# Scoring the first two heads of the second attention together on one NeuronCore

## The reference

```
def _fox_attend(q, k, v, log_f):
    c = jnp.cumsum(log_f, axis=1)
    ...
        s = jnp.einsum('bqhd,bkhd->bhqk', q_b, k, ...) * (d ** -0.5)
        s = s + cq_b[..., :, None] - ck[:, :, None, :]
        s = jnp.where(kpos[None, :] <= qpos[:, None], s, NEG_INF)
        w = jax.nn.softmax(s, axis=-1).astype(v.dtype)
        return jnp.einsum('bhqk,bkhd->bqhd', w, v)
```

## Time and profile before

| | us |
|---|---|
| median of three runs | 2059.25 |
| lowest and highest | 2057.09, 2059.43 |
| the profiled execution, whole | 2058.62 |
| its span, first to last instruction | 2056.8 |

### The profile page before, as it was taken

How to read it: one execution, slowest core, us unless ns; L and a number is a source line. 1 busy time by engine, 2 the same in 40 slices (tenths; PEclk the granted TensorE clock), 3 DMA queues, 4 the chain that set the end, 5 groups by cost and what they waited for, 6 DMA issues and landing times.

```text
span 2056.8 us, 24737 instructions
## 1 busy us (share of the span) xinstructions
PE 1984.4 (96%) x9280; PEld 1643.0 (80%) x9280; DVE 884.6 (43%) x1218; ACT 307.3 (15%) x596; POOL 1281.9 (62%) x831
## 2 busy tenths in 40 slices
PE   9889999999997999999999999998999899999998
PEld 8778778888886878888788888876787778888886
DVE  3468182243338510373642343375458950000234
ACT  1048120000003100263300000031221120000001
POOL 5488566667764555785576667755453456666675
PEclk9999999999999999999999999999999999999999
DMA  6310333232332222212233223232221123323332
GB/s 209 123 42 1 92 93 102 92 101 93 99 116 62 83 92 83 72 43 71 82 113 100 94 94 101 92 103 72 75 80 54 55 89 95 100 92 101 92 100 74
DMA packets 53410, 181.31 MB, mean 88 GB/s; under 512 B 6553, under 2 KB 9291, under 8 KB 53211
## 3 DMA queue, kind: packets, MB, share of 16 engines
q1 hardware_dynamic: 46512, 165.17, 25.6%
q10 hardware_dynamic: 6826, 15.11, 2.2%
HBM read 176.56 MB, written 3.70 MB: 88 GB/s over the span
## 4 chain that ended last, share of the span: by engine, by line
PE 81%; DVE 11%; POOL 5%; ACT 1%; issue 1%; DMA 0%; POOLq 0%; DVEq 0%
PE PS L571 79%; PE PS L728 1%; POOL WL L483 1%; DVE X L1373 1%; DVE X L1374 1%; POOL WH L480 1%; DVE X L1335 1%; DVE STL L1590 1%; PE PS L793 1%; POOL AQL L489 1%; POOL AKL L489 1%; DVE XTL L1364 1%; POOL PB L512 1%; DVE OT L1619 1%; DVE X L1435 0%
## 5 line engine op out<-in xcount | busy, mean ns | idle before, releaser
L480 POOL TENSOR_SCALAR WH<-RW 128x1024 fp32r<-128x1024 f32 x303 | 359.3, 1186 | 697.0 <-PE PS L571 654.9
L483 POOL TENSOR_TENSOR WL<-RW,WH 128x1024 fp32r<-128x1024 f32 x303 | 770.6, 2543 | 25.3
L571 PE MATMUL PS<-XTH,WH 128*128 128x512 f32 x1168 | 458.4, 392 | 5.5 <-POOL WL L483 2.6
L571 PE MATMUL PS<-XTL,WH 128*128 128x512 f32 x1168 | 456.0, 390 | 0.0
L571 PE MATMUL PS<-XTH,WL 128*128 128x512 f32 x1168 | 455.7, 390 | 0.0
L571 PE MATMUL PS<-WL,HSH 128*128 128x512 f32 x688 | 267.5, 390 | 2.1 <-POOL WL L483 2.1
L571 PE MATMUL PS<-WH,HSH 128*128 128x512 f32 x688 | 267.7, 389 | 0.0
L571 PE MATMUL PS<-WH,HSL 128*128 128x512 f32 x688 | 267.7, 389 | 0.0
L571 PEld LDWEIGHTS PS<-XTH,WH 128*128 128x128 f32 x1168 | 219.9, 188 | 54.3 <-DVE XTL L1364 3.9
L571 PEld LDWEIGHTS PS<-XTH,WL 128*128 128x128 f32 x1168 | 220.0, 188 | 46.4
L571 PEld LDWEIGHTS PS<-XTL,WH 128*128 128x128 f32 x1168 | 220.2, 188 | 44.5
(11 more groups left out here) (311 smaller groups left out, 2364.0 us busy)
## 6 DMA issues: line engine op xcount, KB each, us to landing
RW<-stream SPq DMA_DIRECT2D x303, 512.0 KB, 3.6
BC<-gate_rows SPq DMA_DIRECT2D x16, 256.0 KB, 3.2
G<-gain_rows ACTq DMA_DIRECT2D x5, 512.0 KB, 4.2
XS<-xt ACTq DMA_DIRECT2D x4, 512.0 KB, 7.9
X<-x ACTq DMA_DIRECT2D x1, 2048.0 KB, 12.0
G<-bias_vecs ACTq DMA_DIRECT2D x4, 512.0 KB, 5.6
out<-X SPq DMA_DIRECT2D x4, 512.0 KB, 2.6
bias_rows<-QM ACTq DMA_DIRECT2D x1, 1536.0 KB, 6.9
```

What stands on the lines that cost most here:

```text
L480: pool.tensor_scalar(WH[:, j % WS, :], RW[:, j % RAW, :], 1.0, 1.0, ALU.mult, ALU.mult).then_inc(hi_split, 1)
L483: pool.tensor_tensor(WL[:, j % WS, :], RW[:, j % RAW, :], WH[:, j % WS, :].bitcast(F32), ALU.subtract).then_inc(lo_split, 1)
L571: return pe.matmul(o, a, b, start=start, stop=stop)
```

## The change

The second attention no longer opens with `qk(16)`, six fillers and `qk(17)`. A new function `first_pair` issues both heads' scores: for each tile and each of the three products, head 16's matmul (rows 0 to 63) and then head 17's (rows 64 to 127). Head 16 writes banks 0 to 2 as before, head 17 banks 3 to 5, and the mask matmuls come four at a time. It waits for `E_FOX`, which the scores did not before, since banks 4 and 5 still hold the values. `qk(18)` now waits for head 16's masks in place of head 17's, and `turn(16)`, which writes banks 3 to 5, for head 17's. DVE's mask reads head 17 from bank 3 on. The fillers between the heads go, those behind them write bank 6. The first attention is as it was.

```diff
+def score_bank(h):
+    return 3 if h == FOX0 + 1 else 0
...
-                if h:
+                if h == FOX0 + 2:
+                    pe.wait_ge(masked, 4 * (h - 1))
+                elif h:
                     pe.wait_ge(masked, 4 * h)
...
+            def first_pair():
+                s = item_slot(FOX0)
+                pe.wait_ge(evac, E_FOX)
+                pe.wait_ge(staged, staged_count(FOX0))
+                heads = [(slice(0, HD), 0), (slice(HD, P), 3)]
+                for step, (i, _) in enumerate(CAUSAL_ORDER):
+                    n = (i + 1) * P
+                    bank, col = CAUSAL_S[i]
+                    q = slice(i * P, (i + 1) * P)
+                    for j, (a, b) in enumerate(((AQH, AKH), (AQL, AKH), (AQH, AKL))):
+                        for rows, base in heads:
+                            mm(PS[:, base + bank, col:col + n], a[rows, s, q], b[rows, s, 0:n], j == 0, False)
+                    if step % 2:
+                        for e, (_, base) in enumerate(heads):
+                            for j, _ in CAUSAL_ORDER[step - 1:step + 1]:
+                                bank, col = CAUSAL_S[j]
+                                diagonal = slice(col + j * P, col + (j + 1) * P)
+                                x = mm(PS[:, base + bank, diagonal], IDENT_R[:, :], TRI_R[:, :], False, True)
+                                done = {(0, 3): 1, (0, 2): 2, (0, 1): 1, (1, 2): 3, (1, 1): 1}.get((e, j))
+                                if done:
+                                    x.then_inc(scored, done)
...
             def turn(h):
+                if h == FOX0:
+                    pe.wait_ge(masked, 4 * (h + 2))
...
-                qk(first)
-                occupy(3, 6)
-                qk(first + 1)
-                occupy(3, 5)
+                if first == 0:
+                    qk(first)
+                    occupy(3, 6)
+                    qk(first + 1)
+                    occupy(3, 5)
+                else:
+                    first_pair()
+                    occupy(6, 5)
...
-                    x = ve.tensor_tensor_reduce(out=probs(h)[:, at:at + n], in0=PS[:, bank, col:col + n],
+                    x = ve.tensor_tensor_reduce(out=probs(h)[:, at:at + n],
+                                                in0=PS[:, score_bank(h) + bank, col:col + n],
```

## The result

The changed kernel took 2060.89 us (median of 20 runs, 2056.57 to 2063.83) against 2057.23 us before (20 runs beside it, 2054.71 to 2059.43). The ratio is 1.0015, 95% interval 1.0009 to 1.0022: slower by 3.1 us, between 1.9 and 4.5. The forecast was 2057.2 us, which was meant as 1.4 us saved from 2058.62 us, with a range up to 2060.2 us. Those 2058.62 us were a single execution that lies 1.4 us above the median of 20. The profiled execution of the changed kernel took 2059.60 us.

A forecast was written before the change was run, and what follows sets the result against it. PE was taken as the bound, busy 1984.4 of 2056.8 us, with waits at the second attention's opening. Saving 2.2 us less 0.8 for the clock gave 1.4, from 2058.62 to 2057.2 us; range 2054.7 to 2060.2.

The forecast's parts named there:

- Start on the values' copy: First scores of the second attention: they wait for the values' copy and start at about 850.55, 0.12 us later.
- Overlap of the halves: Paired scores of heads 16 and 17 on PE: a pair goes in the time of one product.
- The hold of NB until POOL's subtraction ends: DVE after head 16's masks: the second NB operation still takes 1.13 us, ready at 856.22.
- ACT late in place of DVE: At head 16's reciprocal: ACT ends last, DVE 0.3 us before it; reciprocal at 858.6 in place of 860.81.
- The gap: PE before head 16's transposes: 3.0 us open with nothing to fill them.
- A fall of the clock on it: PE's granted clock in its new wait before head 16's transposes: falls to half, expected at 3 in 4.
- the length of the fall: Half clock from the wait before head 16's transposes: 3.4 us, making turn 17 0.5 to 1.5 us later.
- the slack of 0.55: PE before turn 17: its work ends at 866.4, 0.55 us ahead of the possible start at 866.97.
- the 2.2 us saved: Head 16's reciprocal and, through POOL, turn 17: both 2.2 us earlier, before any clock loss.
- the slower rival: Opening of the second attention: clock stays low past qk(19), 2.0 us slower, 2060.6 us; chance 1 in 10.
- Later stages: Behind the attention: nothing changed, but a low stretch of 3.4 us more or less is worth 1.7 us either way.

The follow-up runs named there:

- e3_before_no6: The kernel before without the six fillers between the first two heads of its second attention, nothing else; ratio 1.0021 to the kernel before.
- e2_serial: The changed kernel with all scores of head 16, then all of head 17 in its own banks, no fillers between; ratio 1.0026 to the kernel before.
- f4_before_swap: The kernel before with only POOL's normalise 17 moved ahead of its cut of pair 2; ratio 1.0002 to the kernel before.
- e1_fill12: The changed kernel with twelve more fillers between the scores of head 18 and the transposes of head 16; ratio 0.9993 to the kernel before.
- f1_half12: The changed kernel with twelve fillers of 64 rows in the gap before the transposes of head 16; ratio 1.0006 to the kernel before.
- f3_serial_mid: The changed kernel with head 16 whole, then head 17, three fillers between and five before head 16's transposes; ratio 1.0014 to the kernel before.

## Why the prediction was wrong

**The steps up to the reciprocal held.** Start on the values' copy: yes. Overlap of the halves: yes, mask groups at S + 1.19 and 2.87 us (worked out 1.17 and 2.83). The hold of NB until POOL's subtraction ends: yes, though it was the first of the two operations and not the second. ACT late in place of DVE: yes, the reciprocal at S + 8.20 (8.05). The gap: 2.93 us (3.0). A fall of the clock on it: yes. The Trainium skill (TensorE: Matmul & The Clock Gate, LDWEIGHTS) has 107 ns for a weight load, as the prediction says. In the trace of before each load of AKH with AQH took 182 ns or more, and the pairs went side by side all the same.

**The step that failed is the length of the fall.** I wrote that "a low stretch of 3.4 us beginning in the gap would cover turn 16 (+1.1 us) and part of qk(19) (up to +0.9 us)". It lasted 13.6 us and covered turn 16 (+0.94), all of qk(19) (+2.23) and the five fillers (+1.1): 4.3 us. Less the slack of 0.55 and the 2.2 us saved, turn 17 came 1.5 us later (S + 20.28 against 18.74), and its transposes cost another 0.5: 2.08 us. This is the slower rival, which I priced at 2.0 us and gave 1 in 10. Its sum comes near the 2.08 us of the opening partly by luck, since two errors cancel: it had qk(19) at +1.6 us (measured 2.23) and the transposes of 17 at +1.1 (measured 0.5). I had taken 3.4 us from two low stretches that each held fillers, five or six matmuls on all rows. In e3_before_no6, without its six, the stretch of before is 10.2 us long. The trace of before had shown that length too, and I overlooked it: two stretches of 10.2 us, each begun in an idle wait of PE (8.90 and 8.65 us). They are shown by their clock, then by the first matmul after the wait:

```profile
654.90:665.10 10.20, 5.12 (x12) 0.50 0.18 51
1395.60:1405.80 10.20, 5.84 (x14) 0.50 0.17 51
```

```profile
659.98 0.80 PE L571 MATMUL PS<-WH,EH 128*128 128x512 f32 x1 [8.90 <-DVE EL L1444]
...
1399.96 0.79 PE L571 MATMUL PS<-WH,EH 128*128 128x512 f32 x1 [8.65 <-DVE EL L1444]
```

So 3.4 us was not a fixed length in that trace. What ends a stretch stays open: five fillers did not end the one in e2_serial.

**A term was mis-sized too.** The 2.2 us of saving were taken against an execution of before that had a low stretch in its own opening. At full clock the order of before has its reciprocal at S + 8.84 (f4_before_swap), so the change saves 0.64 us there and not 2.2. The other 1.5 us (10.38 - 8.84) were the price of the low stretch. The runs point the same way: over the 93 runs of the kernel before, a straight line gives 1.52 us per 0.001 of mean clock. Set against this line, the changed kernel's 20 runs are 0.9 us faster than before at the same clock, and e1_fill12's 0.8 us. This is an estimate. The changed kernel's clocks (0.985 to 0.990) lie mostly below the range of before (0.989 to 0.992), and f4_before_swap, which shares before's opening, lies 0.5 us off the line. At 0.989, where both kernels have runs, the changed one is 0.8 us faster (3 runs against 27). The changed kernel's mean clock is 0.0028 lower, which by the line costs 4.3 us; 4.3 - 0.9 = 3.4 us, where 3.1 (1.9 to 4.5) was measured. So the new order gains something below 1 us, and by this estimate loses four to five times that by the clock.

**Later stages.** In the two profiled executions they are alike: 10.2 us at half clock near 1396 us and 3.4 us near 1618 us in both. In others they differ (e1_fill12's stretch at 1612 us lasted 6.8 us). That this makes the spread of the runs is likely, and was not tested.

What stays open: which property of PE's work lets the clock fall and ends a low stretch, and why the clock stays full in some runs and falls in others of the same kernel (f1_half12, f3_serial_mid).

## What to carry to other kernels

A filler beside a bank conflict may look like waste that the conflict excuses; it can be what keeps TensorE's clock. When a change frees time on TensorE in such a place, try full-row work in the gap: here 4 to 12 fillers did it, and it may cost a few runs to find how many are needed. And before a saving is read off one execution, look at the granted clock of that very stretch: part of what seems to be the order's cost may be the clock's.

## What the hardware showed that I had not expected

- Half clock for 13.6 us with PE busy without a pause, on 64-row products, fillers and transposes (f1_half12), and for 20.4 us in e2_serial.
- Twelve 64-row matmuls of 512 columns in the gap left 5 of 12 runs low, four of 128 rows 3 of 11, twelve of 128 rows 1 of 11, none 16 of 20. These are too few runs to tell the first three apart.
- Products on the two halves of the rows ran fully side by side, also at 512 columns: six of them in 0.81 us.
- A VectorE operation on 4 columns (0.17 us) took 1.25 us because a GpSimd subtraction had started 0.05 us earlier.
